# Final norm of a two-layer encoder step: two of five scale-and-shift steps go from VectorE to ScalarE and GpSimd, and one shift is placed ahead of the last sum

## The reference

```python
def _layernorm(x, g, b):
    mu = jnp.mean(xf, axis=-1, keepdims=True)
    xc = xf - mu
    var = jnp.mean(xc * xc, axis=-1, keepdims=True)
    return (xc * lax.rsqrt(var + EPS) * g + b)

# end of _odd_layer
o = (o.reshape(b, s, SB_W) * jax.nn.silu(g)) @ w_out      # 1024 x 1024
y = _layernorm(ALPHA * x + o, ln_g, ln_b)
```

## Time and profile before

| | before |
|---|---|
| median of 3 runs | 869.32 us (866.99 to 869.53) |
| profiled execution, its own time | 869.3 us |
| its span, first to last instruction | 867.5 us |
| PE busy | 829.4 us (96%) |
| DVE busy | 527.5 us (61%) |
| ACT busy | 413.0 us (48%) |
| POOL busy | 63.5 us (7%) |

### The profile page before, as it was taken

The page is one execution under the profiler, slowest core; times in us unless marked ns, Lnnn a source line. Parts: engine busy times, 40 slices in busy tenths (PEclk is TensorE's granted clock), DMA queues, the critical chain, the costliest instruction groups (busy, mean ns, idle before and its releaser), DMA issues.

```text
span 867.5 us, 17101 instructions
## 1 busy us (share of the span) xinstructions
PE 829.4 (96%) x6676; PEld 707.8 (82%) x6676; DVE 527.5 (61%) x1056; ACT 413.0 (48%) x945; POOL 63.5 (7%) x94
## 2 busy tenths in 40 slices
PE   6999999999999999999999999999999999999994
PEld 6996687878888888677899998888888888877673
DVE  3265346655565657667833466666566776777867
ACT  4233443343444456432224555754675555785710
POOL 2120000000000000001210010001000100000002
PEclk9999999999999999999999999999999999998998
DMA  6631212211323333413133334233333333343203
GB/s 225 152 105 50 61 44 65 64 39 31 129 65 106 105 100 134 139 59 138 49 117 104 117 104 136 88 105 117 114 99 100 118 130 111 100 136 106 73 22 121
DMA packets 67389, 86.25 MB, mean 99 GB/s; under 512 B 6000, under 2 KB 53904, under 8 KB 67312
## 3 DMA queue, kind: packets, MB, share of 16 engines
q1 hardware_dynamic: 63568, 74.47, 27.1%
q0 software_dynamic: 3744, 10.70, 3.9%
HBM read 74.25 MB, written 10.90 MB: 98 GB/s over the span
## 4 chain that ended last, share of the span: by engine, by line
PE 71%; issue 18%; DVE 4%; ACT 3%; POOL 2%; DMA 1%; DVEq 0%; SPq 0%; POOLq 0%; ACTq 0%
PE turn L932 25%; PE pair L932 14%; PE value L932 13%; PE proj L932 11%; PE turn L970 2%; POOL rstd L905 2%; PE turn L1147 1%; PE proj L970 1%; PE value L970 1%; DVE w_lo L1575 1%; PE value L1147 1%; PE proj L1147 1%; PE pair L970 1%; DMA x_sb<-in_x_prompt_dram 0%; ACT w_hi L1345 0%
## 5 line engine op out<-in xcount | busy, mean ns | idle before, releaser
L1575 DVE TENSOR_TENSOR w_lo<-stage,w_hi 128x512 fp32r<-128x512 f32 (+1 forms) x144 | 97.0, 682 | 109.1 <-ACT w_hi L1345 108.9
L932 PE MATMUL turn<-w_hi,xT_hi 128*128 128x256 f32 (+2 forms) x406 | 127.3, 314 | 0.3 <-DVE x_sb L1817 0.3
L932 PE MATMUL turn<-w_hi,xT_lo 128*128 128x256 f32 (+2 forms) x406 | 123.2, 303 | 0.0
L932 PE MATMUL turn<-w_lo,xT_hi 128*128 128x256 f32 (+2 forms) x406 | 123.1, 303 | 0.0
L1345 ACT CAST w_hi<-stage 128x512 fp32r<-128x512 f32 (+1 forms) x144 | 87.2, 615 | 30.0 <-PE turn L932 8.5
L932 PEld LDWEIGHTS turn<-w_hi,xT_hi 128*128 128x128 f32 x406 | 78.1, 192 | 3.6 <-DVE x_sb L1817 0.5
L932 PEld LDWEIGHTS turn<-w_hi,xT_lo 128*128 128x128 f32 x406 | 77.9, 192 | 3.1
L932 PEld LDWEIGHTS turn<-w_lo,xT_hi 128*128 128x128 f32 x406 | 78.2, 193 | 2.7
L932 PE MATMUL value<-w_hi,xT_hi 128*128 128x256 f32 (+2 forms) x196 | 62.8, 320 | 3.0 <-DVE w_lo L1575 3.0
L1425 ACT ACTIVATE work<-pair,peak 128x512 f32<-128x512 f32 (+4 forms) x80 | 41.0, 517 | 45.5 <-DVE peak L1676 45.4
L1687 DVE TENSOR_TENSOR_SCAN probs<-probs 128x512 f32<-128x512 f32 (+4 forms) x80 | 60.9, 794 | 1.6
(11 more groups left out here) (527 smaller groups left out, 2024.5 us busy)
## 6 DMA issues: line engine op xcount, KB each, us to landing
stage<-in_w_in_odd_dram SPq DMA_DIRECT2D x64, 256.0 KB, 2.6
stage<-in_w_in_even_dram SPq DMA_DIRECT2D x44, 256.0 KB, 2.8
k_c<-in_cache_sb_k_dram SPq DMA_DIRECT2D x32, 256.0 KB, 3.4
v_c<-in_cache_sb_v_dram SPq DMA_DIRECT2D x32, 256.0 KB, 2.9
x_sb<-in_x_prompt_dram SPq DMA_DIRECT2D x8, 512.0 KB, 4.3
mlaK<-in_cache_diff_k_dram SPq DMA_DIRECT2D x8, 512.0 KB, 3.9
mlaK<-in_cache_diff_v_dram SPq DMA_DIRECT2D x8, 512.0 KB, 4.4
stage<-in_w_out_even_dram SPq DMA_DIRECT2D x16, 256.0 KB, 2.7
```

The costliest lines, as they stand in the source:

```text
L932: return nc.tensor.matmul(o, l, r, start=first, stop=last)
L1575: v.tensor_tensor(piece(w_lo[:, sec % 2, words]), piece(stage[:, n % STAGES, :]), piece(w_hi[:, sec % 2, words].bitcast(F32)), ALU.subtrac ...
```

## The change

In the tail the order of the jobs becomes: sum 3, norm 3, sum 2, norm 2, shift 3, sum S, shift 2, norm S, sum 1, norm 1, shift S, shift 1, sum 0, norm 0, shift 0. The sums and the norms keep their order; shift 3 and shift S leave DVE; shift 1 now stands ahead of the last sum.

The shifts of tiles 3 and S are split. ScalarE multiplies the tile by its power in place (128x1024), and GpSimd then adds the shift row in place (TENSOR_TENSOR, 128x1024, reads `x_sb` and `v_n`, both in SBUF). GpSimd's queue is then: power 3, power 2, add 3, power S, power 1, add S, power 0. SP stores tiles 3 and S after their adds; its stores keep the order 3, 2, S, 1, 0. The semaphore `ln_done` now counts only the shifts that DVE does, and a power that reuses a slot of `rstd` waits for whoever read the slot last (`scaled` for ScalarE, `ln_done` for DVE).

```diff
-    tail = [("out", 1, 2, 3, 1), ("ln", 1, 3)]
-    for t, u in ((2, 3), (S_TILE, 2), (1, S_TILE), (0, 1)):
-        tail += [("out", 1, 2, t, 1), ("shift", 1, u), ("ln", 1, t)]
-    jobs += tail + [("shift", 1, 0)]
+    jobs += [("out", 1, 2, 3, 1), ("ln", 1, 3), ("out", 1, 2, 2, 1), ("ln", 1, 2), ("shift", 1, 3)]
+    jobs += [("out", 1, 2, S_TILE, 1), ("shift", 1, 2), ("ln", 1, S_TILE), ("out", 1, 2, 1, 1), ("ln", 1, 1), ("shift", 1, S_TILE)]
+    jobs += [("shift", 1, 1), ("out", 1, 2, 0, 1), ("ln", 1, 0), ("shift", 1, 0)]
     return jobs
+SHIFTED_AWAY = (("shift", 1, 3), ("shift", 1, S_TILE))
...
+        shift_no = ordinal(("shift",), lambda j: j not in SHIFTED_AWAY)
+        away_no = ordinal(("shift",), lambda j: j in SHIFTED_AWAY)
+        ln_jobs = list(ln_no)
...  SP
+                    if job in away_no:
+                        sp.wait_ge(away_done, away_no[job])
+                        sp.dma_start(y, x_sb[:, t, :]).then_inc(stored_y, 16)
+                    elif n < len(shift_no):
                         sp.wait_ge(ln_done, n)
...  GpSimd, job "ln"
-                        n = ln_no[job] - 2
-                        pool.wait_ge(ln_done, n)
+                        reader = ("shift",) + ln_jobs[ln_no[job] - 3][1:]
+                        if reader in away_no:
+                            pool.wait_ge(scaled, away_no[reader])
+                        else:
+                            pool.wait_ge(ln_done, shift_no[reader])
...  GpSimd
+                elif job in away_no:
+                    x_ = x_sb[:, job[2], :]
+                    pool.wait_ge(scaled, away_no[job])
+                    nc.gpsimd.tensor_tensor(x_, x_, gains1[1], ALU.add).then_inc(away_done, 1)
...  ScalarE
+                elif job in away_no:
+                    n = ln_no[("ln",) + job[1:]]
+                    act.wait_ge(gained, n)
+                    act.wait_ge(pow_out, pow_no[("ln",) + job[1:]])
+                    nc.scalar.mul(x_sb[:, job[2], :], x_sb[:, job[2], :], rstd[:, n % 2, :]).then_inc(scaled, 1)
...  VectorE
-                elif kind == "shift":
+                elif kind == "shift" and job not in away_no:
```

More of the change, by code:

```diff
@@ L574, in trunk_kernel @@
         stats_done, gained = sem("stats_done"), sem("gained")
+        scaled, away_done = sem("scaled"), sem("away_done")
         stored_y = sem("stored_y")
@@ L829, in _ @@
                 if kind == "shift" and job[1] == 1:
-                    t, n = job[2], ln_no[("ln",) + job[1:]]
+                    t, n = job[2], shift_no.get(job)
                     y = y_p[t] if t < PT_TILES else y_s
-                    if n < len(ln_no):
+                    if job in away_no:
+                        sp.wait_ge(away_done, away_no[job])
+                        sp.dma_start(y, x_sb[:, t, :]).then_inc(stored_y, 16)
+                    elif n < len(shift_no):
                         sp.wait_ge(ln_done, n)
```

## The result

The changed kernel takes 871.27 us (median of 15 runs, 868.92 to 873.32), the kernel before 868.67 us (15 runs, 866.68 to 870.87). The ratio is 1.0029, 95% interval 1.0018 to 1.0039: 2.5 us slower, just at the bound of 0.3% and surely not faster. The profiled execution took 871.44 us with a span of 869.7 us, against 869.3 and 867.5.

What follows compares the result with a forecast made beforehand. The prediction took DVE's pace in the tail as the bound: -1.2 without contention, +1.58 and +2.32 for shifts held up by GpSimd's adds, together +2.7 us, giving 872.0 us; range 868.0 to 873.6.

Steps and rivals of the forecast that it cites:

- What bounds the tail: From 841.61 to the last shift's end at 862.72 the kernel goes at DVE's pace, 7.5 us beyond PE's end.
- The count without contention, -1.2: DVE's tail: three rounds lose 0.98 us each, shift 1 and a wait come back; the last shift ends 1.2 us earlier.
- 0.58 of open wait ahead of shift 1: In the count without contention, DVE comes free 0.58 us before shift 1 can start, waiting for the power of tile 1.
- The add's price, 2.38 by two passes: Each GpSimd add takes two DVE passes of 1.19, 2.38 us, between bounds of 1.19 and 3.57.
- The inference from the powers: GpSimd's 128x1 powers take 1.51 us, not 0.53; they stand still 0.98 us until DVE's gain step is through.
- The reverse direction: While a GpSimd add runs, a DVE gain or shift waits for its end; sums and statistics don't.
- rival 1: GpSimd does not hold DVE up: 1.2 us less, 868.1 us; chance 0.18.
- The two meetings, 1.58 and 2.32: On DVE, shift 2 waits 1.58 us for the end of add 3, shift 1 waits 2.32 us for add S.
- Who wins the second meeting: After power 1, add S starts on GpSimd at 856.83, before DVE's shift 1, free at 856.89; shift 1 loses 2.32 us.
- rival 2: Shift 1 on DVE goes before add S, and the gain of tile 0 waits 0.54: +0.9 us, 870.2; chance 0.08.
- ScalarE and the stores hide: ScalarE's multiply, 1.06 us by the nearest row, and SP's stores add nothing while the adds end before 860.
- Rival 3: Each GpSimd add costs three passes or more, 3.57 us: +5.1 us, 874.4; chance 0.08.

Runs made afterwards that it cites:

- old order: Changed kernel with the two shifts off DVE, but the job order of the kernel before; tail 10.28 us, ratio 1.0030 against the kernel before.
- Experiment 6: Kernel before, but ScalarE copies the gain row into PSUM, where DVE's gain steps of layer 1 read it; tail 7.45 us, ratio 0.9988.
- experiment 1: Changed kernel, but ScalarE copies the shift row into PSUM, where DVE's three shifts read it; tail 6.80 us, ratio 0.9987 against the kernel before.
- experiment 2: Changed kernel, but each GpSimd add is replaced by a memset of 3072 SBUF elements, which reads no SBUF; tail 6.82 us, one run.
- experiment 5: Changed kernel's order with all shifts on DVE: tail 8.62 us, ratio 1.0017; and its offload in the order of before: 10.28 us, 1.0030.
- experiment 3: Changed kernel, but add S on GpSimd also waits until shift 1 on DVE is done; tail 8.68 us, ratio 0.9999 against the kernel before.
- experiment 8: Changed kernel with gain and shift rows in PSUM: tail 5.86 us, ratio 0.9973; with shift 2 also off DVE: 5.23 us, 0.9966.
- adds in halves: Changed kernel, but each of GpSimd's two adds is done as two instructions of 128x512; tail 8.69 us, one run.

## Why the prediction was right

The forecast was 872.0 us, +2.7 us; measured are 871.27 us, +2.5 by the ratio and +2.23 in the tail. Most of what 872.0 is too high comes from its base, the median of 3 runs (869.32), where 15 runs have 868.67. By its steps:

- **What bounds the tail.** Right: PE ends where it did, 854.72 + 0.39. In every kernel of the table PE's last matmul starts 13.2 us after the first sum of the tail, so the tails differ by DVE's and GpSimd's queues alone.
- **The count without contention, -1.2.** Measured by itself as -1.13 with the shift row in PSUM and -1.11 with GpSimd only writing. The 0.58 of open wait ahead of shift 1 was 0.58 by starts, 0.50 as recorded idle time.
- **The add's price, 2.38 by two passes.** 2.40 and 2.34 as recorded; by starts, where a power follows at once (old order), 2.35 and 2.29. The number came out, but its reason was a guess between bounds: no run shows that an add there is two passes of 1.19, and a memset of 3072 elements took 2.67, 0.89 for 1024. With the sum at twice the add's price, hitting it within 0.04 us was in part luck. The Trainium skill (GPSIMD Engine Reference, Performance versus the Vector engine) has 4497 ns for 2048 elements; half of that, 2.25, as an estimate, is a little low.
- **The inference from the powers.** 1.51 - 0.53 = 0.98 was read as a power standing still behind DVE. Experiment 6 shows the power without it at 0.54. (Of the three rows, one is a power of the tail.)
- **The reverse direction, which no row of before showed.** It was assumed, and rival 1 held the case that it fails. Experiments 1, 2 and 5 show it, and rival 1 fell at shift 2, 2.60 us from 848.98. The runs agree with the Trainium skill's rule (SBUF — State Buffer, Who interferes with whom) in both directions, and also in that a GpSimd instruction that only writes does not conflict. "To its end" holds to within 0.2 us: DVE was let in 0.17 to 0.19 before an add's recorded end.
- **The two meetings, 1.58 and 2.32.** They cost 1.35 and 2.03. Both terms were sized 0.2 to 0.3 too high, mainly for two reasons: an add lets DVE in before its recorded end (add 3 ends at 850.50; DVE's next start, at 851.51, less its own 1.18, is 850.33: 0.17 before), and GpSimd started each add 0.03 before the recorded end of the power ahead of it, where I had it 0.03 after. Sum: -1.13 + 1.35 + 2.03 = 2.25, for a tail of +2.23.
- **Who wins the second meeting.** Add S by 0.13 us (856.50 against 856.63), as forecast; 0.09 and 0.03 had been the estimates. Forced the other way (experiment 3), +0.75 for rival 2's +0.9.
- **ScalarE and the stores hide.** Yes: the multiply takes 1.15 us for 1.06 and tile S is ready 1.8 us ahead of its add; from the last shift's end to the end of the span it is 4.8 us before and after.
- **Rival 3** (an add of three passes) fell with the adds' 2.4 us.

On the bound of 0.3% the prediction left slower and same nearly even, and the ratio's interval of 1.0018 to 1.0039 still does.

## What to carry to other kernels

Before work is moved from VectorE to GpSimd, ask what each of the two reads while the other runs: if both read SBUF, and VectorE's instruction has two SBUF inputs, they do not run beside each other, and a pass saved on VectorE (1.18 us here) buys a wait of up to a whole pass of GpSimd (2.0 of 2.4 us). A row that is used again and again can be kept in free PSUM banks by an idle ScalarE for 1.0 us; VectorE reads it there at the same 1.27 us and the conflict is gone: the same offload and order then turned from +2.2 us to -2.1 us in the tail (experiment 8). Such a wait has no releaser in the profile; look for one line and shape with two durations, and for a busy time that rises when work was taken away.

## What the hardware showed that was not expected

- A wait of this kind is inside the instruction's recorded duration, on both engines, and stands in no list of waits. The prediction had read this from the powers and held it possible for DVE. Of the 1.51 us of each power of layer 1, nearly two thirds were waiting.
- Where two instructions were free at about the same time, the one recorded 0.03 us earlier (845.98 against 846.01) went first, and the other stood for 2.2 us.
- A waiting instruction of the other engine goes in between two that stand back to back in one queue (adds in halves; in the old order the gain, let in at 848.19 by its next start less 1.19, ahead of the power of 848.33).
- A semaphore wait that is long fulfilled cost DVE about 0.07 us ahead of the join. It did not everywhere: the wait added ahead of shift 2 in experiment 1 left it at 0.61 behind the statistics.
- The tail's length repeated to 0.01 us between two executions whose ends lay 2 us apart.
